# Rows of the normed activations 520 instead of 512 elements apart in SBUF

## What is computed

```python
def rms_norm_2(x, g):
    xf = x.astype(jnp.float32)
    y = xf * lax.rsqrt(jnp.mean(xf * xf, axis=-1, keepdims=True) + NORM_EPS)
    return (y * g.astype(jnp.float32)).astype(x.dtype)

def swiglu(h, w_in, w_out):
    g, u = jnp.split(h @ w_in, 2, axis=-1)
    return (jax.nn.silu(g) * u) @ w_out

def ffn_step(s, g, shift, scale, gate, w_in, w_out):
    return s + 0.5 * gate * swiglu(modulate(rms_norm_2(s, g), shift, scale), w_in, w_out)
```

## Time and profile before

| what | value |
|---|---|
| median of 3 runs | 2441.07 us (2436.27 to 2443.59) |
| span of the profiled execution | 2431.8 us |
| TensorE matmuls busy | 2286.2 us (94%), 13542 matmuls |
| VectorE busy | 1481.2 us (61%) |
| ScalarE busy | 836.9 us (34%) |
| GpSimd busy | 178.6 us (7%) |
| mean granted TensorE clock | 0.960 of 2.4 GHz |
| read from HBM | 340.93 MB, 141 GB/s over the span |

### The profile page before, as it was taken

One profiled execution on the slowest core, in us unless ns is written; L12 is line 12 of the kernel. 1 busy time (PEld: TensorE's weight loads), 2 busy tenths in 40 slices (PEclk: granted clock), 3 DMA queues, 4 the chain that ended last, 5 costly groups with the idle time before them and its releaser, 6 DMA issues. The chain is left out here.

```text
span 2431.8 us, 36081 instructions
## 1 busy us (share of the span) xinstructions
PE 2286.2 (94%) x13542; PEld 2034.7 (84%) x13542; DVE 1481.2 (61%) x2237; ACT 836.9 (34%) x1137; POOL 178.6 (7%) x222
## 2 busy tenths in 40 slices
PE   7998999999999899999669999989999998989998
PEld 7888999988999788888558888878888887858998
DVE  4636776454777777588777867773333345375555
ACT  4424334333534432222232212232212233264443
POOL 0110000110000010000311000010000001100000
PEclk9989999998999999999779999999999999999999
DMA  5403675321565455555125555432222233212453
GB/s 197 148 35 135 208 236 184 119 100 41 196 226 205 163 196 179 168 190 177 48 100 194 179 175 182 163 131 87 91 99 96 75 106 104 87 36 103 170 194 121
DMA packets 66867, 343.12 MB, mean 141 GB/s; under 512 B 7264, under 2 KB 10592, under 8 KB 44000
## 3 DMA queue, kind: packets, MB, share of 16 engines
q1 hardware_dynamic: 46048, 266.50, 31.7%
q0 software_dynamic: 20736, 75.51, 9.8%
HBM read 340.93 MB, written 1.05 MB: 141 GB/s over the span
## 5 line engine op out<-in xcount | busy, mean ns | idle before, releaser
L644 PE MATMUL gpt<-xn_hi,w_hi 128*128 128x512 f32 (+2 forms) x2656 | 886.4, 334 | 31.4 <-DVE xn_lo L1931 25.0
L645 PE MATMUL gpt<-xn_lo,w_hi 128*128 128x512 f32 (+2 forms) x2656 | 881.5, 332 | 0.0
L646 PE MATMUL gpt<-xn_hi,w_lo 128*128 128x512 f32 (+2 forms) x2656 | 881.3, 332 | 0.0
L1402 DVE TENSOR_TENSOR w_lo<-raw,w_hi 128x2048 fp32r<-128x2048 f32 (+4 forms) x289 | 569.0, 1969 | 299.6 <-ACT w_hi L1045 298.2
L1045 ACT ACTIVATE w_hi<-raw 128x2048 fp32r<-128x2048 f32 (+4 forms) x292 | 481.8, 1651 | 399.9 <-PE gpt L646 354.4
L644 PEld LDWEIGHTS gpt<-xn_hi,w_hi 128*128 128x128 f32 x2656 | 506.1, 191 | 79.2 <-DVE xn_lo L1931 25.7
L645 PEld LDWEIGHTS gpt<-xn_lo,w_hi 128*128 128x128 f32 x2656 | 506.2, 191 | 45.5
L646 PEld LDWEIGHTS gpt<-xn_hi,w_lo 128*128 128x128 f32 x2656 | 506.1, 191 | 45.4
L644 PE MATMUL gpt<-mid_hi,w_hi 128*128 128x512 f32 (+2 forms) x1016 | 343.3, 338 | 2.5 <-DVE w_lo L1402 1.3
L646 PE MATMUL gpt<-mid_hi,w_lo 128*128 128x512 f32 (+2 forms) x1016 | 342.3, 337 | 0.0
L645 PE MATMUL gpt<-mid_lo,w_hi 128*128 128x512 f32 (+2 forms) x1016 | 342.3, 337 | 0.0
(11 more groups left out here) (277 smaller groups left out, 1859.9 us busy)
## 6 DMA issues: line engine op xcount, KB each, us to landing
raw<-in_up_a SPq DMA_DIRECT2D x72, 1024.0 KB, 4.9
ada_w<-in_ada POOLq DMA_DIRECT2D x144, 512.0 KB, 3.8
raw<-in_up_b SPq DMA_DIRECT2D x60, 1024.0 KB, 4.9
raw<-in_down_a SPq DMA_DIRECT2D x48, 768.0 KB, 4.2
raw<-in_down_b SPq DMA_DIRECT2D x48, 640.0 KB, 3.8
raw<-in_win SPq DMA_DIRECT2D x20, 1024.0 KB, 4.9
raw<-in_qkv SPq DMA_DIRECT2D x12, 1024.0 KB, 4.9
raw<-in_wout SPq DMA_DIRECT2D x8, 1024.0 KB, 5.3
```

The source lines that it names most:

```text
L644: mm(o, w_hi[b][:, j, :], hi(k), start=(k == 0), stop=False)
L645: mm(o, w_hi[b][:, j, :], lo(k), start=False, stop=False)
L646: last = mm(o, w_lo[b][:, j, :], hi(k), start=False, stop=(k == kt - 1))
L1402: V.tensor_tensor(w_lo[b][:, 0:tiles, :], raw[b][:, 0:tiles, :], w_hi[b][:, 0:tiles, :].bitcast(F32), ALU.subtract).then_inc(lo_ready, 1)
```

## The change

The rows of `xn_hi` and `xn_lo` become 520 elements (2080 bytes) apart instead of 512 (2048 bytes). The last 8 elements of a row are never written or read. `sb` also gets a parameter for the alignment, which nothing passes and whose value stays 32 bytes. No instruction is added, removed or moved on any engine. What differs in the program is addresses, and the shape of eight access patterns: the pooling's four ScalarE and four VectorE instructions that write two rows at once go over 2 x 2 x 256 elements in place of 4 x 256, because the four stretches are no longer evenly spaced.

```diff
+XN_ROW = T2 + 8
...
-        def sb(name, shape, dt=F32, where=ctx):
-            return where.enter_context(nc.sbuf_tensor(name, shape, dt))
+        def sb(name, shape, dt=F32, where=ctx, align=32):
+            return where.enter_context(nc.sbuf_tensor(name, shape, dt, align_bytes=align))
...
-        xn_hi = sb("xn_hi", [P, KT, T2], F32R)
-        xn_lo = sb("xn_lo", [P, KT, T2], F32R)
+        xn_hi = sb("xn_hi", [P, KT, XN_ROW], F32R)
+        xn_lo = sb("xn_lo", [P, KT, XN_ROW], F32R)
...
+        def dif4(g):
+            return dif[:, g % 2, :, :].rearrange("p (k c) n -> p k c n", c=2)
...
-                gemm(S_POOL // 2 + g // 2, g % 2, 2, 2, lambda k: xn_hi[:, 2 * g + k, :], lambda k: xn_lo[:, 2 * g + k, :], T2)
+                gemm(S_POOL // 2 + g // 2, g % 2, 2, 2, lambda k: xn_hi[:, 2 * g + k, 0:T2], lambda k: xn_lo[:, 2 * g + k, 0:T2], T2)
...
-                A(xn_hi[:, 2 * g:2 * g + 2, :].rearrange("p k (c n) -> p (k c) n", c=2), dif[:, g % 2, :, :], ACT.Copy)\
+                A(xn_hi[:, 2 * g:2 * g + 2, 0:T2].rearrange("p k (c n) -> p k c n", c=2), dif4(g), ACT.Copy)\
                     .then_inc(y_h, 1)
...
-                V.tensor_tensor(xn_lo[:, 2 * g:2 * g + 2, :].rearrange("p k (c n) -> p (k c) n", c=2), dif[:, g % 2, :, :],
-                                xn_hi[:, 2 * g:2 * g + 2, :].rearrange("p k (c n) -> p (k c) n", c=2).bitcast(F32),
+                V.tensor_tensor(xn_lo[:, 2 * g:2 * g + 2, 0:T2].rearrange("p k (c n) -> p k c n", c=2), dif4(g),
+                                xn_hi[:, 2 * g:2 * g + 2, 0:T2].rearrange("p k (c n) -> p k c n", c=2).bitcast(F32),
                                 ALU.subtract).then_inc(pool_ready, 1)
```

## The result

Four runs of the changed kernel gave 2447.66, 2456.26, 2456.72 and 2458.18 us, a median of 2456.49, against 2439.73 for four of the kernel before. The ratio is 1.0058, with a 95% interval from 1.0038 to 1.0078: slower by about 14 us, with an interval from 9 to 19. The span of the profiled execution is 2446.0 us against 2431.8, at the same mean granted clock of 0.960.

The account below looks back on a forecast made before the run. TensorE was taken as the bound: matmuls times the distance between starts. Terms +21.8 - 4.4 + 0 + 0 = +17.4 us gave a span of 2449.2 and a median of 2458.5 us; 8-in-10 range 2431 to 2467.

Parts of the forecast that it names:

- 512 columns: 3456 matmuls over `xn`: distance from 226.7 to 233 ns, +21.8 us, bounds -7.6 and +26.6 us.
- upper bound from `mid`: `xn` matmuls with 512 columns would take at most the 234.4 ns of `mid`, which bounds the term at +26.6 us.
- 256 columns: 2304 matmuls over `xn`: distance from 120.0 to 118.1 ns, -4.4 us, bounds -4.6 and 0.
- 272 columns: 2064 matmuls over `xn`, at 125.3 ns: no change, 0 us, bounds -3.7 and +0.6 us.
- `cn` rows: Rows 1088 bytes apart, 125.6 ns, taken as nearest to the new `xn` for the 272-column forecast of 0.
- Pooling: Four ScalarE and four VectorE instructions get one more dimension with the same elements: 0 us; 0.5 us if each grew 5%.
- Control: `mid`, whose offsets modulo 512 do not change, should stay at 234.4 ns.
- regular state: Steady 226.7 ns at 512 columns, 120.0 at 256, with rows and weight tiles at 128 modulo 512; lost after the change.
- unsettled stretch: First `xn` matmuls with 512 columns after another form or in a first slot, at 232 ns, before settling at 226.7.
- no change: Rival, chance 0.20: something else, such as distance from the weights, sets the pace; `xn` stays at 226.7 and 120.0, time 2441.
- Faster: Rival, chance 0.20: new offsets thin collisions of weight load and moving read; 512 columns at 224.5 ns, -12 to -16 us together.
- Half of it: Only odd rows, at 32 modulo 64, slow to 234 ns; 230 on average, +12 us less 4.4, 2449.

Follow-up runs that it names:

- lo_256_on: Against the kernel before, `xn_lo` alone begins 256 bytes further on, rows still 2048 bytes apart: 2436.4 us, ratio 0.9983 (0.9967 to 0.9999).
- the sweep: TensorE alone, zeros as output, blocks of 96 matmuls behind different predecessors: 256 columns at offset 192 took 117.8 ns behind 512 columns, 113.3 behind 256, both at 0.

## Why the prediction was right, step by step

The direction, the place of the cost and the size held: 2458.5 us forecast, 2456.49 measured, and +17.4 us forecast against +14.2 between the profiled executions. That the time came within 2 us is in part luck: the forecast added 9.3 us to the span as what lies around a run's instructions. That is 1.7 us for every run; the rest is how far the median lies above the profiled execution, and it happened to be much the same after the change (10.5 us from span to median).

- *512 columns.* Forecast 233 ns and +21.8 us; measured 232.6 (232.5 by all starts) and 3456 x 5.8 = +20.0 us. The term was sized 1.8 us too large, by taking a value just under `mid`. The upper bound from `mid` was sound: `mid` sits at offset 160, the dearest of the eight. Of the 96 in the first slots, put at 232 by the forecast, some run at 1.2 GHz and take 427 ns in both kernels, which changes nothing in the sum.
- *256 columns.* Forecast -4.4 us; measured 2304 x -1.6 = -3.7.
- *272 columns.* Forecast 0; measured 2064 x -0.3 = -0.6. The `cn` rows were the right neighbours.
- *Pooling.* Forecast 0; the instructions kept 1057 and 1222 ns, and TensorE's wait for them went from 25.0 to 24.3 us.
- *Control.* `mid` stayed at 234.4 with 512 columns. With 256 it became about 0.6 ns faster by its starts without stalls (118.1 to 117.5), some 0.7 us that I had not counted; its offset is the same. The traces of the other kernels say which it is. In `lo_256_on` `mid` lies at the very addresses of the changed kernel, and there it kept 118.2 over all. In the kernel before, single stages of `mid` had already run at 117.4 and others at 118.5 to 118.6. So the 512 bytes by which `mid` moved have no part in it; it has two values at one offset too. That what ran before it chooses between them, as in the sweep, is likely but not shown for `mid`.

The terms as measured add up to 20.0 - 3.7 - 0.6 - 0.7 = +15.0 us, against 14.2 in span. (All steady distances of the two traces, taken together, give +14.7.)

The step that failed is the reason given for the cost, not a number. The prediction said that the regular state needs rows and weights alike modulo 512 and is lost because "no offset lasts longer than the hi-lo-hi of one tile". The runs showed in its place that with 512 columns each offset modulo 256 has its own distance (repeats agree within 1.0 ns), that even rows at the wrong offset are as slow (233.4) as the uneven ones, and that the uneven ones pay about the mean over the offsets: 232.1, 117.9 and 125.4 ns in the table against 232.6, 118.4 and 125.0 measured. (At 256 columns the mean is 118.5 if offset 192 counts with its 117.8; the trace does not tell which applies.) The hi and lo rows' distance of 256, which the prediction counted into the disorder, costs nothing. That 232 came out of both is partly luck: the unsettled stretch of the earlier trace rows and the mean over offsets are near each other.

Of the rivals, "no change" rested on the tensors' distance from the weights, and `mid` at 128 refuted it. "Faster" expected 224.5 ns when collisions thin out; nothing tried with 512 columns went under 226.7. It was right that leaving 0 pays with 256 columns, where the gain can be 6.7 ns. "Half of it" expected a step at 32 modulo 64, but offsets 128 and 192, both multiples of 64, are as dear as 32.

The rule from the Trainium skill's page "TensorE: Matmul & The Clock Gate", section "Wait — 56ns, not 53.3ns?", has N / 2.4 GHz plus 2.5 ns warm and N / 1.2 GHz cold. The cold part agrees with the trace, 426.7 ns. The warm part does not agree for these fp32r matmuls with a weight load each: 6.7 ns on top of 256 / 2.4 GHz is the best that any run here shows for 256 columns, and 13.3 on top for 512. What inside the chip makes two read streams that lie 32 bytes differently cost 7 ns more is not shown by any of these runs.

## What to carry to other kernels

In a kernel whose TensorE is busy throughout, divide the time between first and last start of a line by the matmuls between them, for every moving tensor and length, and compare with columns over clock: two tensors with the same instructions and different distances point to their addresses. For fp32r matmuls with a weight load each, set the moving rows' offset from the weight tiles (modulo 256 bytes here) by a gap tensor or a start column, per length, and keep row distances a multiple of 256 bytes. Then read the distance again in every stage of the kernel itself: a value from a sweep can be one of two. Look also at which stages now wait for weights, since part of the gain can end there.

## What the hardware showed that was not expected

- The distance between fp32r matmuls at the full clock depends on the offset between moving rows and weight tiles modulo 256 bytes (and on that of `w_hi` from `w_lo` and of hi from lo rows): 226.7 to 234.3 ns with 512 columns over multiples of 32, up to 238 at an offset of 4; 113.3 to 120.1 with 256, 123.4 at 4.
- It depends on the offset between the two, not on either address, and it is there with all other engines idle. At 1.2 GHz it is gone: 427 ns at offset 0, at 16 and over the uneven rows.
- The cheapest offset changes with the length: 0 for 512 columns, 112 or 192 for 256, 112, 160 or 192 for 272, 64 for 448 (200.0 ns, 202.7 at 0) of the three tried there. With 384 columns offsets 0, 32 and 64 all gave 173.3 ns, 128 and 192 gave 176.0 and 176.7. With 128 columns 0, 32 and 64 all gave 111.7.
- One placement can have two steady distances: with 256 columns 117.8 and 113.3 ns at offsets 64 and 192, 118.7 and 113.3 at 16, 118.6 and 117.4 at 160 (`mid`); with 272 columns 126.7 and 123.3 at 112. At 64 and 192 the sweep shows that what ran before chooses.
